# Smaller first pieces of x and of the first weights at the beginning of a two-block transformer kernel

## The chip, the core and the metric

The kernel runs on one core of a Trainium2 chip. The metric is the time of one execution in device microseconds; a profile of one execution shows what each engine did in it. TensorE multiplies, VectorE, ScalarE and GpSimd do the rest, and SyncE here only issues DMAs, as ScalarE and GpSimd can too. A matmul stands in the profile as a weight load (PEld) and a multiplication (PE).

## What is computed

The program is two transformer blocks over 256 rows of 1024 columns. The change touches only the very first product, the input projection of the mLSTM mixer: x (256 x 1024) times the weights `w_in` (1024 x 3080), of which the beginning takes columns 0 to 255 and the eight gate columns.

```python
def mlstm_mixer(x, w_in, gate_b, conv_w, norm_g, w_out):
    proj = x @ w_in
    qk = jax.nn.silu(causal_dwconv(proj[..., :nqk], conv_w))
    v = proj[..., nqk:nqk + nv]
    o = proj[..., nqk + nv:nqk + nv + D_MODEL]
    gates = proj[..., nqk + nv + D_MODEL:].astype(jnp.float32) + gate_b.astype(jnp.float32)
    ...
def first_block(x, mem, mlstm_w_in, ...):
    kv = (mem @ mem_w_kv).astype(jnp.float32)
    ...
            y = mlstm_mixer(x, mlstm_w_in[j], mlstm_gate_b[j], mlstm_conv_w[j],
                            mlstm_norm_g[j], mlstm_w_out[j])
    ...
```

## The kernel before

Every product is split for precision: a factor is rounded to a high part (`WH`, `XH`), and the rest is kept as a low part (`WL`, `XL`); the product is WH·XH + WL·XH + WH·XL, three matmuls for each pair of blocks. The 1024 rows of the contraction are eight blocks of 128. Rounding the high part is a cast, the low part is a subtraction.

All weights come as a list of chunks of 1 MB, each through one of four buffers `RAW`. SyncE issues the chunks in the order of the list; a chunk from number 4 on waits until VectorE has made the low part of the chunk four places ahead. ScalarE casts each chunk (`hi_to`, line 1254), VectorE makes its low part (`lo_to`, line 1948), TensorE multiplies. Each engine's program is written out by hand as a Python function (`tensor`, `scalar`, `vector`, `gpsimd`, `sync`); the engines run their own instructions in order and are tied by counted semaphores.

The beginning is treated apart. x, turned so that its columns lie on partitions (`in_x_t`, into `S`, eight blocks of 256 columns), and chunk 0 of the weights (`in_w_in_first`, into `RAW[0]`, eight blocks of 256) come in four quarters of two blocks, 256 KB each:

- ScalarE issues the first two quarters of the weights (line 1275), SyncE all four of x (line 3073), the gate columns (3075), the last two quarters of the weights (3077), and then chunk 1 (3068).
- ScalarE casts each quarter of x to `XH` (1279), the gate columns to `GH` (1283, 1284), and the last quarter of the weights (1287).
- VectorE casts the first three quarters of the weights (1974), and for each quarter makes the rest of the weights (1978) and the rest of x (1989); once the rest of the gate columns (1984).
- TensorE first runs 15 matmuls on a block of zeros (587), whose product is not used. In `first()` it then takes for each quarter WH·XH, WL·XH, and WH·XL of the quarter before it (`blocks`, line 540, four matmuls each), with the same for the gate columns (`gate`, line 546, two for a quarter; in quarter 1 four, for quarters 0 and 1). That makes 72 matmuls of 256 columns. `second()` follows with chunk 1, in matmuls of 512 columns.

GpSimd loads a mask once the last quarter's rest of x is made (line 2926).

## Time and profile before

| | us |
|---|---|
| median of 3 runs | 938.74 |
| lowest and highest | 938.50, 938.77 |
| the profiled execution | 938.65 |
| its span, first to last instruction | 937.0 |
| TensorE busy | 929.6 |
| VectorE busy | 713.8 |
| ScalarE busy | 528.1 |

The profiled execution lasts 1.65 us longer than its span, since the span leaves out what lies around the instructions. Busy times are sums over the whole span, which has stages of different kinds; which engine sets the end in a stage is read from the waits in it. Times in the views are counted from the span's start. The ends of matmuls are modelled and overlap, so TensorE's pace is read from starts.

### The profile page before, as it was taken

To read this page: it belongs to the slowest core of one execution; us is meant where nothing else is said; L and a number is where in the kernel's file an instruction comes from. 1 tells how busy PE (TensorE), PEld (TensorE's weight loads), DVE (VectorE), ACT (ScalarE), POOL (GpSimd) and SP (SyncE) were. 2 spreads that over 40 slices of the span, in tenths; PEclk is the share of its full clock that TensorE was granted. 3 is DMA by queue.
4 is the path that set the end of the run, shared out by engine and by line. 5 is a ranking of instruction groups with operands and counts; after the bars stand their busy time and mean duration, and the time that the engine had idled before them with its cause. 6 is when DMAs were issued, how large, how long until landed. Compare 5 with 4: busy or idle time off the path is not lost.

```text
span 937.0 us, 12963 instructions
## 1 busy us (share of the span) xinstructions
PE 929.6 (99%) x4989; PEld 801.4 (86%) x4989; DVE 713.8 (76%) x1002; ACT 528.1 (56%) x757; POOL 60.6 (6%) x98
## 2 busy tenths in 40 slices
PE   9999999999999999999999999999999999999997
PEld 8889888988888888889888888888888888888886
DVE  6987778788888776787788877678779886555575
ACT  5867563636655555455275555556576665454543
POOL 0000211001000002100100000002100000000020
PEclk9999999999999999999999999999999999999999
DMA  9795475457988885374399888773733475656521
GB/s 328 235 369 181 135 241 180 164 180 246 321 289 290 287 296 190 105 274 136 130 321 333 288 295 285 252 261 118 247 119 107 136 246 185 221 180 199 173 78 45
DMA packets 109659, 202.98 MB, mean 217 GB/s; under 512 B 4332, under 2 KB 75264, under 8 KB 106272
## 3 DMA queue, kind: packets, MB, share of 16 engines
q1 hardware_dynamic: 106000, 189.15, 59.5%
q0 software_dynamic: 3168, 12.24, 3.8%
q8 instruction: 40, 0.66, 0.3%
q10 hardware_dynamic: 432, 0.79, 0.2%
q14 instruction: 19, 0.16, 0.1%
HBM read 201.09 MB, written 1.06 MB: 216 GB/s over the span
## 4 chain that ended last, share of the span: by engine, by line
PE 98%; DVE 0%; DMA 0%; ACT 0%; issue 0%; POOLq 0%; POOL 0%; ACTq 0%
PE WB L387 23%; PE WB L393 12%; PE YB L414 12%; PE YB L421 12%; PE YB L429 12%; PE YB L490 6%; PE WB L414 3%; PE WB L421 3%; PE WB L429 3%; PE YB L931 1%; PE WB L531 1%; PE WB L789 1%; PE WB L367 1%; PE WB L374 1%; PE WB L370 1%; PE YB L904 1%
## 5 line engine op out<-in xcount | busy, mean ns | idle before, releaser
L1948 DVE TENSOR_TENSOR wl<-raw,wh 128x2048 fp32r<-128x2048 f32 (+1 forms) x143 | 329.0, 2307 | 99.5 <-ACT wh L1254 95.0
L1254 ACT CAST wh<-raw 128x2048 fp32r<-128x2048 f32 (+1 forms) x147 | 280.0, 1907 | 37.1 <-PE YB L429 14.8
L387 PE MATMUL WB<-XS,wh 128*128 128x512 f32 x960 | 230.9, 390 | 0.0
L387 PEld LDWEIGHTS WB<-XS,wh 128*128 128x128 f32 x960 | 178.1, 188 | 36.1 <-DVE U L2619 0.4
L393 PEld LDWEIGHTS WB<-XS,wl 128*128 128x128 f32 x960 | 124.8, 191 | 5.7
L393 PE MATMUL WB<-XS,wl 128*128 128x256 f32 x960 | 126.5, 283 | 0.0
L414 PE MATMUL YB<-wh,FHT 128*128 128x512 f32 x344 | 106.6, 391 | 0.0
L421 PE MATMUL YB<-wl,FHT 128*128 128x512 f32 x344 | 106.2, 390 | 0.0
L429 PE MATMUL YB<-wh,FLT 128*128 128x512 f32 x344 | 106.1, 389 | 0.0
L1479 ACT COPY U<-WB 128x256 f32<-128x256 f32 x102 | 33.1, 376 | 125.8 <-PE WB L393 125.8
L421 PEld LDWEIGHTS YB<-wl,FHT 128*128 128x128 f32 x344 | 64.6, 188 | 13.8
L429 PEld LDWEIGHTS YB<-wh,FLT 128*128 128x128 f32 x344 | 64.6, 188 | 13.7
L414 PEld LDWEIGHTS YB<-wh,FHT 128*128 128x128 f32 x344 | 62.1, 189 | 10.5
L1935 DVE SCALAR_TENSOR_TENSOR raw<-raw,AR 128x1024 f32<-128x1024 f32 x48 | 56.7, 1219 | 0.0
L490 PE MATMUL YB<-wh,XS 128*128 128x512 f32 x160 | 44.2, 402 | 0.0
L414 PE MATMUL YB<-wh,XS 128*128 128x512 f32 x136 | 42.8, 401 | 0.0
L421 PE MATMUL YB<-wl,XS 128*128 128x512 f32 x136 | 41.5, 391 | 0.0
L429 PE MATMUL YB<-wh,XS 128*128 128x512 f32 x136 | 41.4, 390 | 0.0
L1470 ACT CAST XS<-WB 128x512 fp32r<-128x512 f32 x16 | 9.4, 587 | 46.6 <-PE WB L531 46.6
L490 PEld LDWEIGHTS YB<-wh,XS 128*128 128x128 f32 x160 | 28.7, 188 | 6.1 <-DVE XS L2242 0.6
L429 PEld LDWEIGHTS YB<-wh,XS 128*128 128x128 f32 x136 | 25.5, 188 | 5.5
L421 PEld LDWEIGHTS YB<-wl,XS 128*128 128x128 f32 x136 | 25.5, 188 | 5.4
(399 smaller groups left out, 1205.3 us busy)
## 6 DMA issues: line engine op xcount, KB each, us to landing
raw<-in_mlp_w SPq DMA_DIRECT2D x64, 1024.0 KB, 5.4
raw<-in_w_ada_t SPq DMA_DIRECT2D x24, 1024.0 KB, 5.0
raw<-in_mlstm_w_in SPq DMA_DIRECT2D x11, 1024.0 KB, 8.2
raw<-in_w_ffn_down SPq DMA_DIRECT2D x11, 1024.0 KB, 5.1
raw<-in_w_ffn_gate SPq DMA_DIRECT2D x10, 1024.0 KB, 5.4
raw<-in_w_ffn_up SPq DMA_DIRECT2D x10, 1024.0 KB, 5.7
raw<-in_mem_w_kv SPq DMA_DIRECT2D x8, 1024.0 KB, 8.1
raw<-in_xattn_wq SPq DMA_DIRECT2D x8, 1024.0 KB, 7.0
```

The lines of the kernel that those rows point to most:

```text
L367: e.matmul(o, H[:, at(k)], xh[:, k, :], start=k == 0, stop=False)
L387: e.matmul(W[:, :], H[:, at(k, f)], XS[:, k, :], start=k == 0, stop=False)
L393: p = e.matmul(W[:, 0:256], L[:, at(k, f)], XH[:, k, :], start=False, stop=k == 7)
L414: e.matmul(o, xh[:, k0 + k, tk], pick(H, k), start=start and k == 0, stop=False)
L421: f = e.matmul(o, xh[:, k0 + k, tk], pick(L, k), start=False, stop=stop and low_last and k == a - 1)
L429: f = e.matmul(o, xl[:, k0 + k, tk], pick(H, k), start=False, stop=stop and not low_last and k == a - 1)
L490: f = e.matmul(YB[t][:, :], x[:, k, 128 * t:128 * t + 128], w[ms[n] % NS][:, 512 * (k % 4):512 * (k % 4) + 512], start=start and k == 0, s ...
L1254: f = e.copy(w[:, 0:a * b], raw[:, 0:a * b])
L1470: e.copy(XH[:, 4 * h:4 * h + 4, 128 * t:128 * t + 128], W[:, :].rearrange("p (k c) -> p k c", k=4)).then_inc(act_ln.add(("hi", s, t, h)))
L1479: p = e.copy(o[:, 256 * f:256 * f + 256], bank_of.get(key + (f,), WB[0])[:, 256:512])
L1935: f = e.scalar_tensor_tensor(w, w, 1.0, CROW, ALU.mult, ALU.mult, accum_out=MS[:, c:c + 1])
L1948: f = e.tensor_tensor(L[:, 0:a * b], raw[:, 0:a * b], H[:, 0:a * b].bitcast(F32), ALU.subtract)
```

## The change

x and chunk 0 of the weights now land in four pieces of 1, 1, 2 and 4 blocks (`LANDED`) instead of four of 2, and are rounded and multiplied in five parts of 1, 1, 2, 2 and 2 blocks (`ROUNDED`); the last two parts wait for the same landed piece (`lands`).

- ScalarE issues the first three pieces of the weights (128, 128 and 256 KB), SyncE the four of x (128, 128, 256 and 512 KB), the gate columns behind the third, and the last piece of the weights (512 KB) after all of x.
- ScalarE casts x in five parts, the gate columns behind the third, and the weights' blocks 6 and 7. VectorE casts blocks 0 to 5 of the weights in four parts.
- VectorE's order: high and low of part 0, high and low of part 1, rest of x for blocks 0 and 1 in one operation, high and low of part 2, rest of the gates, rest of x, high and low of part 3, rest of x, low of part 4, rest of x.
- TensorE runs 12 matmuls on zeros instead of 15. In `first()` WH·XL of blocks 0 and 1 follows part 1, and for the gate columns part 2. The 72 matmuls stay.
- GpSimd's load of the mask waits for the fifth part instead of the fourth.

```diff
+        LANDED = (slice(0, 1), slice(1, 2), slice(2, 4), slice(4, 8))
+        ROUNDED = (slice(0, 1), slice(1, 2), slice(2, 4), slice(4, 6), slice(6, 8))
+        lands = (0, 1, 2, 3, 3)
...
-                for q in range(4):
-                    ks = range(2 * q, 2 * q + 2)
+                for q, part in enumerate(ROUNDED):
+                    ks = range(part.start, part.stop)
                     e.wait_ge(*act_front["x", q])
-                    e.wait_ge(*(dve_front["w", q] if q < 3 else w_hi[0]))
+                    e.wait_ge(*(dve_front["w", q] if q < 4 else w_hi[0]))
                     blocks(Ws, 0, WH, XH, ks, start=True)
...
-                    if q > 0:
+                    if q == 1:
+                        e.wait_ge(*dve_front["x", 1])
+                        blocks(Ws, 0, WH, XL, range(0, 2))
+                    if q == 2:
+                        gate(GH, XL, range(0, 2))
+                    if q > 2:
+                        ks = range(ROUNDED[q - 1].start, ROUNDED[q - 1].stop)
                         e.wait_ge(*dve_front["x", q - 1])
-                        blocks(Ws, 0, WH, XL, range(2 * q - 2, 2 * q))
-                        gate(GH, XL, range(2 * q - 2, 2 * q))
...
-            for n in range(15):
+            for n in range(12):
                 p = e.matmul(WB[3][:, 0:256], XL[:, 7, 0:128], XL[:, 7, :], start=True, stop=True)
...
-            for q in range(2):
-                e.dma_start(first_quarter(q), I["w_in_first"][:, 2 * q:2 * q + 2, :]).then_inc(d_first[q], 16)
-            for q in range(4):
-                ks, cs = slice(2 * q, 2 * q + 2), slice(512 * q, 512 * q + 512)
-                e.wait_ge(d_xt[q], 16)
+            for q in range(3):
+                e.dma_start(first_part(LANDED[q]), I["w_in_first"][:, LANDED[q], :]).then_inc(d_first[q], 16)
+            for q, ks in enumerate(ROUNDED):
+                e.wait_ge(d_xt[lands[q]], 16)
                 e.copy(XH[:, ks, :], S[:, ks, :]).then_inc(act_front.add(("x", q)))
...
+            def first_high(q):
+                cs = slice(256 * ROUNDED[q].start, 256 * ROUNDED[q].stop)
+                e.wait_ge(d_first[lands[q]], 16)
+                e.tensor_copy(WH[0][:, cs], RAW[0][:, cs]).then_inc(dve_front.add(("w", q)))
...
-            for q in range(4):
-                ks = slice(2 * q, 2 * q + 2)
+            for q, ks in enumerate(LANDED):
                 e.dma_start(S[:, ks, :], I["x_t"][:, ks, :]).then_inc(d_xt[q], 16)
-                if q == 1:
+                if q == 2:
                     e.dma_start(PC[:, C_WG:C_WG + 64], I["gates"]).then_inc(d_gcols, 16)
-                if q > 1:
-                    e.dma_start(first_quarter(q), I["w_in_first"][:, ks, :]).then_inc(d_first[q], 16)
+            e.dma_start(first_part(LANDED[3]), I["w_in_first"][:, LANDED[3], :]).then_inc(d_first[3], 16)
```

SyncE's DMAs from the start up to chunk 1 (`in_mlstm_w_in`), before:

```order
L3073 DMA S<-in_x_t 128x512 x2
L3075 DMA PC<-in_gates 128x64
L3073 DMA S<-in_x_t 128x512
L3077 DMA raw<-in_w_in_first 128x512
L3073 DMA S<-in_x_t 128x512
L3077 DMA raw<-in_w_in_first 128x512
L3068 DMA raw<-in_mlstm_w_in 128x8x256
```

and now:

```order
L3094 DMA S<-in_x_t 128x256 x2
L3094 DMA S<-in_x_t 128x512
L3096 DMA PC<-in_gates 128x64
L3094 DMA S<-in_x_t 128x1024
L3097 DMA raw<-in_w_in_first 128x1024
L3090 DMA raw<-in_mlstm_w_in 128x8x256
```

The weights of blocks 4 and 5 stood ahead of the last quarter of x; now they are in one DMA with blocks 6 and 7, behind all of x.

VectorE from its first cast of the weights (wh) to the cast of blocks 4 and 5, with what each waits for (`in_first` and `raw_in0` are landings of the weights), before:

```order
L1974 CAST wh<-raw 128x512 [waits in_first0]
L1978 TENSOR_TENSOR wl<-raw,wh 128x512 [waits dve_front]
L1989 TENSOR_TENSOR XS<-S,XS 128x2x256 [waits act_front]
L1974 CAST wh<-raw 128x512 [waits in_first1]
L1978 TENSOR_TENSOR wl<-raw,wh 128x512 [waits dve_front]
L1984 TENSOR_TENSOR FLT<-PC,FHT 128x8x4 [waits act_front]
L1984 TENSOR_TENSOR FLT<-PC,FHT 128x8x4
L1989 TENSOR_TENSOR XS<-S,XS 128x2x256
L1974 CAST wh<-raw 128x512 [waits in_first2]
```

and now:

```order
L1981 CAST wh<-raw 128x256 [waits in_first0]
L1986 TENSOR_TENSOR wl<-raw,wh 128x256 [waits dve_front]
L1981 CAST wh<-raw 128x256 [waits in_first1]
L1986 TENSOR_TENSOR wl<-raw,wh 128x256 [waits dve_front]
L1991 TENSOR_TENSOR XS<-S,XS 128x2x256 [waits act_front]
L1981 CAST wh<-raw 128x512 [waits in_first2]
L1986 TENSOR_TENSOR wl<-raw,wh 128x512 [waits dve_front]
L2003 TENSOR_TENSOR FLT<-PC,FHT 128x8x4 [waits act_front]
L2003 TENSOR_TENSOR FLT<-PC,FHT 128x8x4
L1991 TENSOR_TENSOR XS<-S,XS 128x2x256 [waits act_front]
L1981 CAST wh<-raw 128x512 [waits raw_in0]
```

The first cast of the weights is half as wide, the rest of x comes behind two parts of the weights, and the cast of blocks 4 and 5 now waits for the last landing of chunk 0 (`raw_in0`).

TensorE from the matmuls on zeros up to block 4 (wh and wl are the weights' parts, FHT and FLT those of the gate columns), before:

```order
L587 MATMUL WB<-XS 128x256 x15
L540 MATMUL YB<-XS,wh 128x256 x4
L540 MATMUL YB<-XS,wl 128x256 x4
L540 MATMUL YB<-XS,wh 128x256 x4
L546 MATMUL YB<-XS,FHT 64x256 x4
L540 MATMUL YB<-XS,wl 128x256 x4
L546 MATMUL YB<-XS,FLT 64x256 x4
L540 MATMUL YB<-XS,wh 128x256 x4
L546 MATMUL YB<-XS,FHT 64x256 x2
L540 MATMUL YB<-XS,wh 128x256 x4
```

and now:

```order
L596 MATMUL WB<-XS 128x256 x12
L543 MATMUL YB<-XS,wh 128x256 x2
L543 MATMUL YB<-XS,wl 128x256 x2
L543 MATMUL YB<-XS,wh 128x256 x2
L543 MATMUL YB<-XS,wl 128x256 x2
L543 MATMUL YB<-XS,wh 128x256 x8
L549 MATMUL YB<-XS,FHT 64x256 x4
L543 MATMUL YB<-XS,wl 128x256 x4
L549 MATMUL YB<-XS,FLT 64x256 x4
L549 MATMUL YB<-XS,FHT 64x256 x2
L543 MATMUL YB<-XS,wh 128x256 x4
```

Blocks 0 and 1 are now taken one by one, and the low part of x for them (the first four of the row of eight) comes ahead of blocks 2 and 3. In both, the last row is WH·XH of blocks 4 and 5, with 30 matmuls between the zeros and it.

## Rows read from the trace of the kernel before

**Rows 1.** The page, part 1: busy time of each engine, share, instructions.

```profile
PE 929.6 (99%) x4989; PEld 801.4 (86%) x4989; DVE 713.8 (76%) x1002; ACT 528.1 (56%) x757; POOL 60.6 (6%) x98
```

**Rows 2.** The waits of TensorE, whole span: us in total, times, longest.

```profile
PE WB L587 <- DVE XS L1964: 1.2, 1, 1.2
PE YB L540 <- DVE wh L1974: 0.2, 1, 0.2
```

**Rows 3.** The chain that ended last, 0 to 15 us: start, us, what.

```profile
0.73 3.58 DMA raw<-in_w_in_first
4.34 0.44 DVE wh L1974
4.91 2.61 PE YB L540 x12
...
14.11 0.48 PE YB L540 x4
```

**Rows 4.** Stretches, TensorE: us, busy (instructions), granted clock, DMA share, GB/s.

```profile
5.00:7.00 2.00, 2.00 (x10) 1.00 0.97 298
7.00:9.48 2.48, 2.48 (x22) 1.00 1.01 355
```

**Rows 5.** Weight loads by line, 1:4.6 and 7.8:14 us: xcount, busy, mean ns.

```profile
L587 PEld LDWEIGHTS WB<-XS 128*128 128x128 f32 x15 | 3.3, 327 | 1.2 <-DVE XS L1964 1.2
...
L540 PEld LDWEIGHTS YB<-XS,wh 128*128 128x128 f32 x22 | 3.0, 189 | 0.0
```

**Rows 6.** The timeline of weight loads: start, us, instruction, count.

```profile
5.69 0.97 PEld L540 LDWEIGHTS YB<-XS,wl 128*128 128x128 f32 x4
6.55 0.76 PEld L540 LDWEIGHTS YB<-XS,wh 128*128 128x128 f32 x4
```

**Rows 7.** The timeline of TensorE, two pieces of it.

```profile
9.48 0.63 PE L540 MATMUL YB<-XS,wh 128*128 128x256 f32 x4
...
14.43 3.82 PE L540 MATMUL WB<-XS,wh 128*128 128x512 f32 x16
```

**Rows 8.** The timeline of SyncE: when each DMA is issued.

```profile
2.57 0.43 SPq L3077 DMA_DIRECT2D raw<-in_w_in_first  x1
...
3.51 0.43 SPq L3077 DMA_DIRECT2D raw<-in_w_in_first  x1
```

**Rows 9.** DMAs in flight from 0.9, 1.3, 2.8, 3.7 us: KB, us to landing.

```profile
raw<-in_w_in_first ACTq DMA_DIRECT2D x1, 256.0 KB, 3.6
...
raw<-in_w_in_first ACTq DMA_DIRECT2D x1, 256.0 KB, 4.4
...
raw<-in_w_in_first SPq DMA_DIRECT2D x1, 256.0 KB, 5.5
...
raw<-in_w_in_first SPq DMA_DIRECT2D x1, 256.0 KB, 5.9
```

**Rows 10.** The timeline of VectorE, the casts and rests of the first blocks.

```profile
4.34 0.43 DVE L1974 CAST wh<-raw 128x512 fp32r<-128x512 f32 x1 [1.81 <-DMA raw<-in_w_in_first]
4.80 0.69 DVE L1978 TENSOR_TENSOR wl<-raw,wh 128x512 fp32r<-128x512 f32 x1
...
8.09 0.43 DVE L1974 CAST wh<-raw 128x512 fp32r<-128x512 f32 x1
```

**Rows 11.** Packets of all queues in 2.1:5.6, 5:5.6, 5.8:9.5, 9.5:12.4 us.

```profile
DMA packets 747, 1.14 MB, mean 325 GB/s; under 512 B 208, under 2 KB 208, under 8 KB 747
...
DMA packets 137, 0.13 MB, mean 225 GB/s; under 512 B 79, under 2 KB 79, under 8 KB 137
...
DMA packets 889, 1.29 MB, mean 348 GB/s; under 512 B 62, under 2 KB 459, under 8 KB 889
...
DMA packets 1102, 1.06 MB, mean 365 GB/s; under 512 B 32, under 2 KB 1102, under 8 KB 1102
```

**Rows 12.** The timeline of ScalarE, the last cast of chunk 0 and chunk 1.

```profile
9.48 0.62 ACT L1287 CAST wh<-raw 128x512 fp32r<-128x512 f32 x1
...
13.39 1.04 ACT L1292 CAST wh<-raw 128x1024 fp32r<-128x1024 f32 x1
```

More of the change, by code:

```diff
@@ L551, in first @@
                 Ws = [YB[f][:, 0:256] for f in range(2)]
-                for q in range(4):
-                    ks = range(2 * q, 2 * q + 2)
+                for q, part in enumerate(ROUNDED):
+                    ks = range(part.start, part.stop)
                     e.wait_ge(*act_front["x", q])
-                    e.wait_ge(*(dve_front["w", q] if q < 3 else w_hi[0]))
+                    e.wait_ge(*(dve_front["w", q] if q < 4 else w_hi[0]))
                     blocks(Ws, 0, WH, XH, ks, start=True)
-                    gs = range(0 if q == 1 else 2 * q, 2 * q + 2)
-                    if q > 0:
+                    gs = range(0 if q == 2 else part.start, part.stop)
+                    if q > 1:
                         e.wait_ge(*act_front["gates"])
                         gate(GH, XH, gs, start=True)
-                    e.wait_ge(*(w_lo0[q] if q < 3 else w_lo[0]))
+                    e.wait_ge(*(w_lo0[q] if q < 4 else w_lo[0]))
                     blocks(Ws, 0, WL, XH, ks)
-                    if q > 0:
+                    if q > 1:
                         e.wait_ge(*dve_front["gates"])
                         gate(GL, XH, gs)
-                    if q > 0:
+                    if q == 1:
[5 more added lines that the diff above has]
+                        ks = range(ROUNDED[q - 1].start, ROUNDED[q - 1].stop)
                         e.wait_ge(*dve_front["x", q - 1])
-                        blocks(Ws, 0, WH, XL, range(2 * q - 2, 2 * q))
-                        gate(GH, XL, range(2 * q - 2, 2 * q))
-                e.wait_ge(*dve_front["x", 3])
+                        blocks(Ws, 0, WH, XL, ks)
+                        gate(GH, XL, ks)
+                e.wait_ge(*dve_front["x", 4])
                 gate(GH, XL, range(6, 8), stop=True).then_inc(pe_front.add("gates"))
@@ L1978, in vector, with first_low, x_low @@
+            def first_low(q):
+                cs = slice(256 * ROUNDED[q].start, 256 * ROUNDED[q].stop)
+                e.wait_ge(*(dve_front["w", q] if q < 4 else w_hi[0]))
                 e.tensor_tensor(WL[0][:, cs], RAW[0][:, cs], WH[0][:, cs].bitcast(F32), ALU.subtract
-                                ).then_inc(w_lo0.add(q) if q < 3 else w_lo.add(0))
+                                ).then_inc(w_lo0.add(q) if q < 4 else w_lo.add(0))
+            def x_low(q, ks):
                 e.wait_ge(*act_front["x", q])
-                if q == 1:
-                    e.wait_ge(*act_front["gates"])
-                    for o, c in ((0, 0), (32, 4)):
-                        p = e.tensor_tensor(GL[:, :, o:o + 4], GRAW[:, :, c:c + 4], GH[:, :, o:o + 4].bitcast(F32),
-                                            ALU.subtract)
-                    p.then_inc(dve_front.add("gates"))
@@ L1987, in vector @@
-                if q == 3:
-                    e.wait_ge(*pe_front["zeros"])
                 e.tensor_tensor(XL[:, ks, :], S[:, ks, :], XH[:, ks, :].bitcast(F32), ALU.subtract
                                 ).then_inc(dve_front.add(("x", q)))
+            first_high(0)
+            first_low(0)
+            first_high(1)
+            first_low(1)
+            x_low(1, slice(0, 2))
+            first_high(2)
+            first_low(2)
+            e.wait_ge(*act_front["gates"])
+            for o, c in ((0, 0), (32, 4)):
+                p = e.tensor_tensor(GL[:, :, o:o + 4], GRAW[:, :, c:c + 4], GH[:, :, o:o + 4].bitcast(F32),
+                                    ALU.subtract)
@@ L1991, in vector @@
+            p.then_inc(dve_front.add("gates"))
+            x_low(2, slice(2, 4))
+            first_high(3)
+            first_low(3)
+            x_low(3, slice(4, 6))
+            first_low(4)
+            e.wait_ge(*pe_front["zeros"])
+            x_low(4, slice(6, 8))
             at[:] = [1, 1]
```

22 lines of the change are left out of this document (7 added, 15 removed).

## The prediction

> **What bounds the kernel now.** I read the page first, then who waited for whom, then the first 20 us piece by piece. The page says that TensorE is busy 99% of the span [rows 1]. That is an average, so I asked what TensorE ever waits for in the 937.0 us: two waits, 1.2 us for the first memset and 0.2 us for the first cast weights [rows 2]. After the first true matmul at 4.91 us it never waits again. So from there the end moves by exactly as much as TensorE's stream is shifted, and nothing later takes a shift back. The question is only where the stream stands when the work of `first()` is over.
>
> The chain at the start [rows 3]: the first quarter of the weights is issued at 0.73 and lands about 3.6 us later, VectorE casts it from 4.34 to 4.78, and the first true matmul starts at 4.91. Then matmuls run back to back into the second chunk, whose first one starts at 14.43 [rows 7]. Their pace has two levels. The granted-clock column prints 1.00 in all these stretches, though 10 matmuls stand in the two microseconds up to 7.0 and 22 in the next 2.5 [rows 4], but the weight loads took 327 ns on average while the 15 dummy matmuls ran and 189 ns after 7.8 us [rows 5], and four load-and-multiply pairs took 0.86 us (the loads that start at 5.69 and at 6.55, [rows 6]) and later 0.47 us [rows 3]: 0.215 against 0.1175 us each. That is 1.2 GHz up to about 7.0 us and 2.4 GHz from there.
>
> So TensorE's order matters in a second way: up to 9.48 it does 30 matmuls (8 of quarter 0, 22 of quarter 1 with the gate columns), and 42 after that (from 9.48 to 14.43, 4.95 us, [rows 7]). At 9.48 it turns to blocks 4 and 5. In the kernel before these had landed with margin: their weights are issued at 2.57 [rows 8] and land 5.5 us later [rows 9], at 8.07; VectorE's cast starts at 8.09 [rows 10]; TensorE wants it at 9.48.
>
> **The change, part by part.**
>
> *Small first pieces.* x and the first weights of block 0 are 128 KB each instead of 256 KB. Before, the first 256 KB of the weights landed 3.6 us after the issue [rows 9], those of x a little earlier. Between 2.1 and 5.6 us all queues together moved 325 GB/s [rows 11], so 256 KB less ahead of the first wait is 0.8 us at most; if the landing is latency and not bytes, it is nothing. I take 0.7. VectorE's cast of 256 columns instead of 512 saves about half of 0.43 us [rows 10], say 0.15. The first true matmul then starts at 4.91 - 0.85 = 4.05, between 3.9 and 4.91. The lower end is set by the dummies: 12 instead of 15 takes 3 x 0.215 = 0.65 us off their end, from about 4.55 to 3.9.
>
> *The order on TensorE.* Blocks 0 and 1 now come singly; the same 30 matmuls stand ahead of blocks 4 and 5 as before (4 + 8 + 18), and 42 stand behind. From 4.05 at the slow step up to 7.0 that is 13 or 14 matmuls, and 16 at 0.1175 follow: TensorE is through with them at 8.9 to 9.0. With a start at 4.91 it would be 9.48 again.
>
> *The order on VectorE.* The second part of x's remainder is now one operation over blocks 0 and 1 after both weight parts. From 3.6 on its row is cast 0 (0.25), rest 0 (0.35), then cast 1 from its landing near 4.35, rest 1 and x rest (0.69 as any of these rests, [rows 10]), which ends near 5.7; TensorE asks for it after 8 matmuls, 4.05 + 8 x 0.215 = 5.77. The cast of blocks 2 and 3 then runs to 6.2 and TensorE wants it at 6.6, since w(2:4) lands as w(1) did before, near 5.6 (issued at 1.2, 4.4 us to landing, [rows 9]). These are all covered, the first by under 0.1 us; that cover gone, it costs the same few tenths, but only ahead of the wait that follows, and so nothing.
>
> *The large last pieces.* Here the change adds a wait. The weights of blocks 4 to 7 are one 512 KB piece, and it stands last of the six DMAs of the beginning on SyncE's queue. Before, blocks 4 and 5 of the weights came ahead of x's last quarter. Now VectorE's cast of them, which TensorE needs at 8.9, waits until blocks 6 and 7 have come as well. The same bytes lie ahead of that last byte as before (1 MB of x, 1 MB of weights, the gates; 512 KB of them on ScalarE's queue in both), and before it landed 5.9 us after its issue at 3.51, at 9.4 [rows 8, 9]. ScalarE's cast of it started at 9.48 [rows 12].
>
> How early can it land now? One bound is the old one, 9.4, or 0.1 to 0.2 later. For the other: in 5.0 to 5.6 the queues moved only 225 GB/s, in 5.8 to 9.5 348, and once one chunk streamed undisturbed, 365 [rows 11]. If the dip and the piece boundaries vanish, 0.6 x 225 + 3.6 x 348 = 1390 KB at 365 GB/s are 3.8 us, so 5.0 + 3.8 = 8.8. There are fewer and longer pieces behind 5.6 us (two of 512 KB where there were four of 256 KB), but the gates' small packets are still there. I take the middle, 9.1.
>
> From landing to matmul the row of the first quarter gives the price: landed 4.33, cast from 4.34, matmul at 4.91 [rows 3, 10], 0.58 us. So blocks 4 and 5 begin at 9.1 + 0.58 = 9.7 instead of 9.48. TensorE stands idle from 8.9 to 9.7. The 0.5 us that the early start brings are given back in that wait, and 0.2 us more.
>
> *Behind the wait.* Queued behind VectorE's waiting cast are its rests of w(4:6), x(4:6), w(6:8) and x(6:8), 0.69 us each [rows 10]: they end at 9.1 + 0.45 + 4 x 0.7 = 12.4. TensorE asks for the first at 9.7 + 6 x 0.1175 = 10.4 (it is there at 10.25), for w(6:8) at 12.5 (there at 11.7) and for the last x at 13.9. All hold. ScalarE casts w(6:8) from 9.2 to 9.8; needed at 11.8. The second chunk's cast, whose second half runs from 13.39 to 14.43 [rows 12], is not later, since its bytes are not; TensorE comes to the first half near 14.6 and to the second 1.8 later.
>
> *What else is moved.* SyncE issues six DMAs ahead of the second chunk instead of seven, so that one is issued some 0.5 us earlier; it queues behind the same bytes, so I count nothing. GpSimd's mask load waits for the last x rest, now some 1 us later; its reader comes tens of us later.
>
> **The sum.** The profiled execution took 938.65 us with a span of 937.0; the median of the runs is 938.74. Shift of TensorE's stream at blocks 4 and 5: 9.7 - 9.48 = +0.2 us; everything behind it moves along: 938.65 + 0.2 = 938.85, or 938.94 from the median. I say 938.9. The bounds of the landing, 8.8 and 9.6, make -0.1 and +0.7; the lower one stops at TensorE's own readiness (8.9 to 9.48); neither leaves 938.5 to 939.4.
>
> **Rivals.**
>
> *The large piece lands early.* If it lands by 8.4, TensorE at 8.95 finds its weights and the whole early start is kept: 9.48 - 8.95 = 0.53 us, 938.1. For it speaks the dip to 225 GB/s, which is lost time between small pieces; against it that even at 365 GB/s throughout I come only to 8.8, which keeps nothing or 0.1. The Trainium skill, "DMA: Bandwidth & Descriptors", Rules for kernel authors, asks for DMAs of 1 MiB or more for the greatest bandwidth; by that rule the long pieces would land early and the short ones late. The rows only show that the rate was higher later, not that the size did it. Chance 0.2 for some gain between 0.1 and 0.5.
>
> *Slower: TensorE's clock falls in the new wait.* The place is the 0.8 us of idleness at 8.9, the first after the rise. If the chip takes it for idleness, the matmuls behind it run at 0.215 again. At the start the low level lasted from 1.2 to 7.0, 5.8 us [rows 2, 4]: in such a stretch 27 matmuls run that would take 3.2 us, so +2.6 and 941.5, slower by 0.3%. It decides from a wait long enough to count, of which no row of before tells, as TensorE never waits there once it is at 2.4 GHz. The Trainium skill, "TensorE: Matmul & The Clock Gate", What's actually happening, says that "the default state is throttled, and activity releases the throttle"; no run here shows a fall in mid-kernel. The wait is short beside the 5.8 us of the rise: chance 0.04. A rise that only comes later than 7.0 costs less, as the wait at 8.9 hides most of it.
>
> *The first pieces land no earlier.* Then the first matmul stays at 4.91, the dummies end 0.65 us earlier into an idle engine, and the 30 matmuls end at 9.48: TensorE still waits until 9.7, and the time is the same 938.9. Chance 0.1; it cannot be told from the forecast by the time, only by the trace.
>
> **How the numbers follow.** Forecast 0.66 at 938.9 (own range 938.5 to 939.4), no earlier landing 0.1 at the same time, gain 0.2 down to 938.1, clock 0.04 at 941.5. The range of 938.1 to 939.5 leaves out the clock case and the tails. A measurement of this kernel can tell about 0.2%, 1.9 us, from no change; every case but the clock's is inside, so: same 0.95, slower 0.04, faster 0.01.
>
> **What would show it.** In the profile after: the first true matmul near 4.05 with a cast of 256 columns ahead of it; a wait of TensorE for the cast of blocks 4 and 5, 0.5 to 1 us long, ending near 9.7, released by VectorE, whose cast in turn waits for the DMA of the first weights; no other wait of TensorE; matmuls at 0.1175 us behind it; the second chunk's first matmul near 14.65 instead of 14.43. I am wrong if the last weight piece lands well before 9.0, if TensorE waits for x's or the weights' rests, or if the loads behind the wait take 327 ns again.

## The result, and the profile after

| | before | after |
|---|---|---|
| median of 9 runs each, us | 938.50 | 942.20 |
| lowest and highest | 938.38, 938.77 | 940.03, 943.71 |
| ratio, 95% interval | | 1.0033 (1.0025 to 1.0042) |
| the profiled execution | 938.65 | 943.71 |

The change makes the kernel slower by 3.7 us in the median. The ratio is estimated from all the runs; the two medians alone would give 1.0039. The forecast was 938.9, with 938.1 to 939.5 as its range; none of the nine runs lies in it. The nine runs after fall into two groups: four at 940.03 to 940.42 with a mean granted clock of 0.998 or more, and five at 942.20 to 943.71 with 0.996 or 0.997. One profile was taken in each group; the second belongs to another execution of the same kernel, told below as e13. One of the ten runs of e15 below took 1323.94 us at a mean granted clock of 0.655, and is in neither its median nor its ratio.

The page of the slower execution, busy time of each engine, which answers to [rows 1]:

```profile
PE 931.6 (99%) x4986; PEld 803.5 (85%) x4986; DVE 714.1 (76%) x1004; ACT 528.4 (56%) x758; POOL 61.0 (6%) x98
```

Its waits of TensorE over the whole span (us in total, times, longest), which answer to [rows 2]:

```profile
PE YB L543 <- ACT FHT L1292: 3.2, 1, 3.2
PE WB L596 <- DVE XS L1972: 1.2, 1, 1.2
```

The shares are within a point of those before. What is new is one line, 3.2 us of waiting in line 543, for ScalarE's cast of the gate columns. The timeline of TensorE (start, us, instruction, count) says where, and answers to [rows 7]:

```profile
3.91 0.77 PE L543 MATMUL YB<-XS,wh 128*128 128x256 f32 x2
...
5.66 0.67 PE L543 MATMUL YB<-XS,wh 128*128 128x256 f32 x4
9.56 1.19 PE L543 MATMUL YB<-XS,wh 128*128 128x256 f32 x4 [3.23 <-ACT FHT L1292]
...
13.53 1.05 PE L543 MATMUL YB<-XS,wh 128*128 128x256 f32 x4
...
19.48 1.78 PE L543 MATMUL WB<-XS,wh 128*128 128x512 f32 x7
```

The first true matmul is at 3.91. After twelve matmuls, all that blocks 0 and 1 give, TensorE has nothing, from 6.3 to 9.56: it waits ahead of blocks 2 and 3, not ahead of blocks 4 and 5, which begin at 13.53. `second()` starts at 19.48 instead of 14.43, 5.05 us late, and the execution ends 943.71 - 938.65 = 5.06 us late.

Who is late there is told first by the chain that ended last (start, us, what), which answers to [rows 3]:

```profile
2.09 7.04 DMA PC<-in_gates
9.14 0.02 issue
9.16 0.22 ACT FHT L1291
```

Then by the timeline of VectorE, its casts of the first weights, of blocks 2 and 3, and of blocks 4 and 5 [rows 10]:

```profile
3.47 0.29 DVE L1981 CAST wh<-raw 128x256 fp32r<-128x256 f32 x1 [0.94 <-DMA raw<-in_w_in_first]
...
8.98 0.43 DVE L1981 CAST wh<-raw 128x512 fp32r<-128x512 f32 x1 [3.44 <-DMA raw<-in_w_in_first]
...
11.74 0.43 DVE L1981 CAST wh<-raw 128x512 fp32r<-128x512 f32 x1 [0.80 <-DMA raw<-in_w_in_first]
```

And by the DMAs of x(2:4), w(2:4), the gate columns and w(4:8), with their KB and us from issue to landing [rows 9]:

```profile
S<-in_x_t SPq DMA_DIRECT2D x1, 256.0 KB, 5.5
raw<-in_w_in_first ACTq DMA_DIRECT2D x1, 256.0 KB, 7.3
PC<-in_gates SPq DMA_DIRECT2D x1, 32.0 KB, 7.0
...
raw<-in_w_in_first SPq DMA_DIRECT2D x1, 512.0 KB, 8.7
```

The weights of blocks 2 and 3 take 7.3 us to land, the gate columns 7.0. The second quarter of the weights, which held the same blocks, took 4.4 [rows 9]. The last piece of the weights takes 8.7 us and lands at 11.71, where the last quarter took 5.9 and landed at 9.46. A landing is sixteen arrivals, each of which counts the DMA's semaphore up by one, and an engine that waits for the count of 16 needs the last. Of the weights of blocks 2 and 3, ten arrivals are in by 5.44, and the other six come at 6.13, 6.36, 6.76, 7.29, 8.38 and 8.96. Before, all sixteen came between 4.97 and 5.58.

Behind the wait the matmuls are slow. Two stretches (us, then busy and count of PE, PEld, DVE, ACT and POOL, then granted clock, DMA share, GB/s), which answer to [rows 4]:

```profile
9.56:15.67 6.11, 6.11 (x29) 6.11 (x30) 4.31 (x9) 2.71 (x5) 0.33 (x1) 0.50 1.09 361
15.95:19.48 3.53, 3.53 (x33) 3.53 (x32) 2.29 (x1) 0.76 (x1) 0.17 (x1) 1.00 1.10 362
```

A group of weight loads in the first of them (count, busy, mean ns), which answers to [rows 5]:

```profile
L543 PEld LDWEIGHTS YB<-XS,wl 128*128 128x128 f32 x8 | 1.9, 330 | 0.0
```

The granted clock is 0.50 in the first stretch, that is 1.2 GHz, and a load takes 330 ns, as the dummy matmuls' loads did before. In the record the clock falls at 8.93, while TensorE still waits, and is back at 15.76. So two things add up. Had the clock stayed, the 18 matmuls of blocks 2 and 3 and the gates would have ended at 9.56 + 18 x 0.1175 = 11.7. Blocks 4 and 5 would have had to wait for their landing, 11.71 + 0.58 = 12.3, and with 42 matmuls in 5.0 us `second()` would have started at 17.3. Of the 5.05 us, then, 2.9 belong to the landings and 2.2 to the clock. This division is worked out, not measured; e11 and e13 show a fall and a late landing each by itself.

### The profile page after: what moved, and what is told of

Read it like the earlier page. It is cut to its first block, busy times and chain, and to the rows that moved or that the text cites. A ratio compares the mean times of both kernels' runs of the same rounds, so it can differ in the third digit from the quotient of the medians.

```text
span 941.9 us, 12960 instructions
## 1 busy us (share of the span) xinstructions
PE 931.6 (99%) x4986; PEld 803.5 (85%) x4986; DVE 714.1 (76%) x1004; ACT 528.4 (56%) x758; POOL 61.0 (6%) x98
## 4 chain that ended last, share of the span: by engine, by line
PE 98%; DMA 1%; DVE 0%; ACT 0%; issue 0%; SPq 0%; POOLq 0%; POOL 0%; ACTq 0%
PE WB L390 23%; PE WB L396 12%; PE YB L417 12%; PE YB L424 12%; PE YB L432 12%; PE YB L493 6%; PE WB L417 3%; PE WB L424 3%; PE WB L432 3%; PE YB L940 1%; PE WB L534 1%; PE WB L798 1%; PE WB L370 1%; PE WB L377 1%; PE WB L373 1%; DMA PC<-in_gates 1%
```

## The experiments

All are compared with the kernel before on the same chips (938.3 to 938.6 in the median). "After" is the changed kernel. The table gives for each profiled execution when the latest of x(2:4), w(2:4) and the gate columns landed (what `first()` needs for its third part), when the last piece of the weights landed, how much all queues moved from 5.0 to 7.5 us, and when `second()` began; then the median of the runs and the ratio with its interval. One profile is one execution, and landings scatter; the medians carry the verdicts.

| kernel | blocks 2, 3 and gates | last weights | GB/s | `second()` | median | ratio |
|---|---|---|---|---|---|---|
| before | 5.84 | 9.46 | 295 | 14.43 | 938.50 | |
| after | 9.14 | 11.71 | 200 | 19.48 | 942.20 | 1.0033 (1.0025, 1.0042) |
| e13 after, again | 6.64 | 10.31 | 227 | 15.93 | 940.15 (one run) | |
| e1 last pieces split | 7.60 | 10.01 | 270 | 16.66 | 939.93 | 1.0016 (1.0006, 1.0025) |
| e2 before, last joined | 7.48 | 10.27 | 210 | 15.88 | 940.15 | 1.0018 (1.0009, 1.0028) |
| e3 matmuls in the wait | 9.48 | 12.12 | 236 | 17.72 | 941.56 | 1.0032 (1.0020, 1.0044) |
| e4 chunk 1 later | 8.03 | 10.62 | 291 | 16.23 | 941.32 | 1.0028 (1.0017, 1.0039) |
| e5 gates by GpSimd | 9.55 | 11.78 | 202 | 19.53 | 944.00 | 1.0059 (1.0044, 1.0074) |
| e6 w(4:8) ahead of x(4:8) | 6.85 | 8.88 | 227 | 15.88 | 940.80 | 1.0027 (1.0018, 1.0037) |
| e7 e1 and e5 together | 7.30 | 9.82 | 307 | 15.02 | 941.84 | 1.0038 (1.0024, 1.0052) |
| e8 x contiguous | 6.50 | 9.81 | 336 | 15.43 | 939.78 | 1.0015 (1.0005, 1.0024) |
| e12 weights contiguous | 7.66 | 10.12 | 293 | 15.74 | 940.03 | 1.0017 (1.0007, 1.0026) |
| e14 both contiguous | 7.20 | 9.93 | 360 | 15.54 | 939.69 | 1.0013 (1.0003, 1.0023) |
| e9 both contiguous, split | 6.85 | 9.42 | 346 | 14.39 | 939.50 | 1.0011 (1.0001, 1.0020) |
| e15 w(2:4) by SyncE | 7.39 | 10.40 | 221 | 16.02 | 940.36 | 1.0024 (1.0014, 1.0033) |
| e10 before, contiguous | 6.95 | 9.41 | 312 | 14.98 | 938.56 | 1.0001 (0.9991, 1.0010) |

In all of these profiles but e1's (0.4) and e9's (0.9), the delay of `second()` against 14.43 agrees within 0.2 us with the delay of the whole execution against 938.65.

### Each half of the change alone: e1 and e2

e1 is after with the last piece cut in two again, so that the small first pieces stand alone.

```diff
-        LANDED = (slice(0, 1), slice(1, 2), slice(2, 4), slice(4, 8))
+        LANDED = (slice(0, 1), slice(1, 2), slice(2, 4), slice(4, 6), slice(6, 8))
...
-        lands = (0, 1, 2, 3, 3)
+        lands = (0, 1, 2, 3, 4)
...
+                if q > 2:
+                    e.dma_start(first_part(ks), I["w_in_first"][:, ks, :]).then_inc(d_first[q], 16)
-            e.dma_start(first_part(LANDED[3]), I["w_in_first"][:, LANDED[3], :]).then_inc(d_first[3], 16)
```

> The changed kernel with its last pieces of four blocks cut into two of two blocks, each with a wait of its own, in the order x(4:6), w(4:6), x(6:8), w(6:8); all else stays. In the profile of the changed kernel the bytes moved fell to 85 to 250 GB/s from 5.0 to 7.5 us, just when x's 512 KB piece began, and blocks 2 and 3 and the gate columns landed at 7.1 to 9.1 us. Theory A (the 512 KB piece of x with its rows of 4 KB fills the rings and slows them): blocks 2 and 3 land near 5.6 again, TensorE waits nowhere after 3.9, the clock does not fall, 938.0 us (0.5 below before). Theory B (chunk 1's DMA, issued 0.5 us earlier, disturbs): here it is issued as late as before, so also near 938. Theory C (the small first pieces, or the third piece of the weights on ScalarE's queue, upset the rings): blocks 2 and 3 land as late as now, 940 to 943 us.

e2 is the kernel before with only its last two quarters joined, of x and of the weights.

```diff
-            for q in range(4):
-                ks = slice(2 * q, 2 * q + 2)
+            for q in range(3):
+                ks = slice(2 * q, 2 * q + 2) if q < 2 else slice(4, 8)
                 e.dma_start(S[:, ks, :], I["x_t"][:, ks, :]).then_inc(d_xt[q], 16)
...
```

> The kernel before with only its last two quarters of x and of the weights joined into pieces of four blocks (512 KB); the first two quarters, the 15 matmuls on zeros and all orders stay. Theory A: the slow stretch comes at 5 to 7.5 us here too; but only what lies behind the first two quarters is late: the weights of blocks 4 to 7 land near 11, TensorE waits about 1 to 2 us at 9.5 us, 940 to 942 us. Theory C: the slow stretch stays away, the last weights land near 9.4, 939.0 to 939.3 us (the wait that the prediction worked out).

Each half costs by itself: 939.93 and 940.15. For e1 theories A and B gave 938.0; it did not come, though there is no large piece in e1 and chunk 1 is issued at 4.48 us, later than before. Seven of its ten runs are at 939.30 to 940.23, the other three at 941.08 to 941.45 with a mean clock of 0.996 or 0.997. e2 came out at the lower end of theory A's 940 to 942, with the joined weights earlier than its 11 us. In e1 TensorE's wait stands at blocks 2 and 3; in e2 it stands once at the gate columns and once at blocks 4 and 5. The waits of TensorE in e1, but for the first memset's:

```profile
PE YB L543 <- DVE wh L1981: 1.3, 1, 1.3
```

And those in e2:

```profile
PE YB L540 <- DVE wh L1974: 0.8, 2, 0.7
PE YB L546 <- ACT FHT L1284: 0.6, 1, 0.6
```

In e2 nothing ahead of the joined pieces was touched, and yet two of the sixteen arrivals of the gate columns came at 7.20 and 7.48, where fourteen had come by 5.83; and the joined weights landed at 10.27, 0.8 later than the last quarter did. So the joining, as e2 does it, neither brings the last piece sooner nor leaves the pieces ahead of it alone. But chunk 1 has two DMAs fewer ahead of it in e2 and is issued at 3.05 instead of 3.99; what the joining does without that is not shown by e2. e4 below holds chunk 1 back in the changed kernel.

### The clock: e3 and e11

e3 fills the wait of after with 24 matmuls on zeros between parts 1 and 2, whose product is not used.

```diff
+                    if q == 2:
+                        for n in range(24):
+                            p = e.matmul(WB[3][:, 0:256], XL[:, 7, 0:128], XL[:, 7, :], start=True, stop=True)
+                        p.then_inc(pe_front.add("zeros"))
                     e.wait_ge(*act_front["x", q])
...
-            p.then_inc(pe_front.add("zeros"))
```

> The changed kernel with 24 more matmuls on zeros between part 1 and part 2, where TensorE stood idle for 3.2 us in its profile. They change no landing. If half of the loss is the clock that falls in the idle stretch (matmuls of 0.2135 us from 8.9 to 15.8 us in the profile, 34 of them instead of 0.1175: some 2.2 to 3 us), the slowest runs of 942 to 944 us go and all lie near 940 to 941. If the clock is no part of it, the spread of 940 to 944 us stays.

The gate columns landed as late as in after's first profile (9.48), but the clock record stays at 1.00 from its rise to the last microseconds, and no run is above 942.03. The last weights landed at 12.12, and `second()` began at 17.72, which is 12.12 + 0.58 + 5.0: the landings' share as worked out above, without the clock's. The zeros themselves cost 24 x 0.1175 = 2.8 us in runs that would not have waited so long, so the lowest run rises from 940.03 to 940.92, and nothing is won on the whole: the ratio is 1.0032 against 1.0033.

e11 is the kernel before with one wait put in: TensorE waits for the landing of chunk 1 ahead of blocks 4 and 5. No DMA is changed.

```diff
                 for q in range(4):
                     ks = range(2 * q, 2 * q + 2)
+                    if q == 2:
+                        e.wait_ge(s_raw[1], 16)
```

> The kernel before with one more wait on TensorE: ahead of blocks 4 and 5 it waits for the landing of chunk 1, at 12.4 us in the profile of before, so it stands idle from 9.5 to about 12.5 while every landing stays as it is. It prices idleness by itself. If the clock stays at 2.4 GHz: 3.1 us, 941.5. If the clock falls in it, matmuls of 0.2135 us follow for some microseconds and the weight loads there take 327 ns: 943 to 945 us, with a spread between runs of 2 us or more.

Its wait of TensorE for chunk 1:

```profile
PE YB L540 <- DMA raw<-in_mlstm_w_in: 3.5, 1, 3.5
```

The stretch behind it, with the granted clock third from the end:

```profile
12.63:18.50 5.87, 5.87 (x27) 5.87 (x28) 2.29 (x1) 1.97 (x2) 0.35 (x1) 0.50 1.10 356
```

And the first matmuls of `second()` in the timeline of TensorE:

```profile
20.37 0.86 PE L540 MATMUL WB<-XS,wh 128*128 128x512 f32 x3
```

Blocks 4 and 5 begin at 12.63 instead of 9.48, so idleness alone is 3.15 us, and 938.5 + 3.15 = 941.65. One of the four runs is there (941.50, clock 0.998). Two are at 943.37 and 944.64 with 0.996 and 0.995; the fourth is at 943.21 with 0.998, and has no profile that would tell why. In the profiled one `second()` is 20.37 - 14.43 = 5.94 us late, 2.8 more than the wait explains. That is the price of the fall by itself, in a kernel whose DMAs are those of before.

### The changed kernel again: e13

> The changed kernel itself, a second look. If late landing of blocks 2 and 3 is its habit, the profile shows TensorE waiting there again, 1 to 3.5 us, with w(2:4) or the gate columns landing at 7.4 or later, and the time is 940 to 940.5 without a fall of the clock and 942 to 944 with one. If the first profile was an odd execution, the wait at blocks 2 and 3 is under 0.5 us and the main wait stands at blocks 4 and 5, 1 to 1.5 us.

Its wait of TensorE, beside that for the memset:

```profile
PE YB L543 <- DVE wh L1981: 1.5, 1, 1.5
```

Its timeline of TensorE, from the first true matmul to `second()`:

```profile
4.01 0.77 PE L543 MATMUL YB<-XS,wh 128*128 128x256 f32 x2
...
8.98 0.39 PE L549 MATMUL YB<-XS,FHT 128*64 128x256 f32 x2
10.91 0.71 PE L543 MATMUL YB<-XS,wh 128*128 128x256 f32 x4 [1.53 <-DVE wh L1981]
...
15.93 3.82 PE L543 MATMUL WB<-XS,wh 128*128 128x512 f32 x16
```

And the stretch from blocks 4 and 5 to `second()`, at a granted clock of 1.00:

```profile
10.91:15.93 5.02, 5.02 (x43) 5.02 (x43) 2.93 (x5) 2.04 (x3) 0.78 (x1) 1.00 1.10 352
```

This is the forecast's own course with one number changed. The matmuls run through blocks 2 and 3 with a pause of 0.13 us by the profile (0.33 by the starts). TensorE is through with the thirty at 9.2, and waits for blocks 4 and 5 alone. Their weights land at 10.31 instead of 9.1, the matmul follows 0.60 later, the clock stays, and the execution is 940.15, 1.5 us slower than before's. Of my two branches the second held: the main wait stands at blocks 4 and 5, with 1.53 us where 1 to 1.5 were expected. The time alone would have fitted the first as well. So the 1.6 us of the four runs without a fall can come from either place.

### What makes the landings late: e4, e5, e6, e7 and e15

Five changes in what stands beside the late pieces. e4 holds back chunk 1, e5 takes the gate columns' short rows off SyncE's queue, e6 sends the weights ahead of x, e7 is e5 with the pieces of e1 and has no further edit, e15 moves w(2:4) from ScalarE's queue to SyncE's.

```diff
+            e.wait_ge(d_xt[3], 16)
             for n in range(1, len(chunks)):
```

> The changed kernel with one more wait on SyncE: chunk 1 and all behind it are issued only when x's last piece has landed. Theory A and C: the slow stretch from 5 to 7.5 us stays, blocks 2 and 3 land late as now, 940 to 943 us, or worse by what chunk 1 is late. Theory B (chunk 1's 1024 short rows per partition group, made ready from 4 us on, slow the rings): the stretch goes, blocks 2 and 3 land near 5.6, the last weights near 9.2, about 939 us.

```diff
-                if q == 2:
-                    e.dma_start(PC[:, C_WG:C_WG + 64], I["gates"]).then_inc(d_gcols, 16)
...
+            e.dma_start(PC[:, C_WG:C_WG + 64], I["gates"]).then_inc(d_gcols, 16)
             e.memset(MH, -0.5).then_inc(po_front.add("mh"))
```

> The changed kernel with the gate columns' DMA (128 rows of 256 bytes) taken out of SyncE's queue: GpSimd issues it at the very start. In every trace so far the packets turn slow at 5.0 us, just when this DMA has run. Theory G (the short rows disturb the rings): the slow stretch at 5 to 7.5 us goes or moves to 3 us, blocks 2 and 3 land by 5.6, and the time falls to 938 to 939 us. Theory X (x's last blocks are read slowly whatever stands ahead): slow packets stay from 5 to 7.5 us, but the gates land early; TensorE still waits for blocks 2 and 3 or for 4 and 5, 939.5 to 942 us. Theory T (something else runs at that time): as X.

```diff
             for q, ks in enumerate(LANDED):
+                if q == 3:
+                    e.dma_start(first_part(ks), I["w_in_first"][:, ks, :]).then_inc(d_first[q], 16)
                 e.dma_start(S[:, ks, :], I["x_t"][:, ks, :]).then_inc(d_xt[q], 16)
...
-            e.dma_start(first_part(LANDED[3]), I["w_in_first"][:, LANDED[3], :]).then_inc(d_first[3], 16)
```

> The changed kernel with the two 512 KB pieces in the other order, weights of blocks 4 to 7 first, then x's. Theory X (reading x is what is slow): the stretch from 5 us runs near 380 GB/s now, and the slow stretch comes behind it, at about 6.3 to 8; blocks 2 and 3 land near 5.6, TensorE then waits for x's blocks 4 and 5 at about 9.5 to 10.5. Theory G and T: the weights' packets are slow from 5 to 7.5 us as x's were, blocks 2 and 3 land at 7 to 9 us, 940 to 943 us.

> Both at once: the last pieces in two of two blocks each, and the gate columns issued by GpSimd. If each of the two (long pieces, short rows) delays the landings by itself, this is the one of the four that beats the kernel before: no wait of TensorE behind 3.9 us, 938.0 us. If the slow stretch has another cause, it waits for blocks 2 and 3 as in the run with the split pieces alone, 939 to 941.5 us.

```diff
-            for q in range(3):
+            for q in range(2):
                 e.dma_start(first_part(LANDED[q]), I["w_in_first"][:, LANDED[q], :]).then_inc(d_first[q], 16)
...
                 if q == 2:
+                    e.dma_start(first_part(ks), I["w_in_first"][:, ks, :]).then_inc(d_first[q], 16)
                     e.dma_start(PC[:, C_WG:C_WG + 64], I["gates"]).then_inc(d_gcols, 16)
```

> The changed kernel with the weights of blocks 2 and 3 issued by SyncE behind x(2:4) instead of by ScalarE. If its place in the row of transfers made it late (ScalarE issues it before x(2:4), and its packets then share the engines with x(2:4) and x(4:8)), it lands within 0.3 us of x(2:4), near 7.1, and the wait shrinks to about 1.3 us: 939.8 to 940.3 and no fall. If the slow stretch of the engines takes whatever is in flight between 5 and 7.5 us, w(2:4) lands at 7.4 to 9 as before and the time stays 940 to 943.

None of the five brings the landings back, so none of these neighbours is the cause by itself. In e4 the queues moved more in the slow stretch, but one of the sixteen arrivals came at 7.31, 8.03 and 10.62 for w(2:4), the gates and w(4:8), 1.1 to 1.7 us behind the fifteenth each time: a better mean rate, the same wait. In e5 the gate columns were in earlier (7.30), and four of the sixteen arrivals of x(2:4) came at 8.42 to 9.07; TensorE waited 3.8 us, the clock fell at 8.30, and all four runs are above 943.7. In e6 the weights landed at 8.88, and then x(4:8) was the late one, at 10.14. e7 shows both pictures in its runs: 939.29 in the profiled one, and 941.50 to 942.70 with a clock of 0.996 or 0.997 in the four others. In e15 x(2:4) was in at 5.54 and w(2:4), right behind it, at 7.20, since one arrival came a full microsecond after the others (6.22). Seven of e15's runs are at 940.03 to 940.68, two at 942.26 and 942.74.

### How the pieces lie in HBM: e8, e12, e14, e9 and e10

In HBM a partition of x and of the first weights is a row of eight blocks, 8 KB, of which a DMA of four blocks reads 4 KB. In these kernels each piece is an array of its own, so that a DMA reads one closed stretch. e8 does it for x, e12 for the first weights, e14 for both, e9 for both with the five pieces of e1, e10 for both in the kernel before. The edit of e8, the others being like it:

```diff
-                e.dma_start(S[:, ks, :], I["x_t"][:, ks, :]).then_inc(d_xt[q], 16)
+                e.dma_start(S[:, ks, :], I[f"x_t{q}"]).then_inc(d_xt[q], 16)
...
+    for q, (a, b) in enumerate(((0, 1), (1, 2), (2, 4), (4, 8))):
+        out[f"x_t{q}"] = out["x_t"][:, a:b]
+    del out["x_t"]
```

> The changed kernel with x laid out in four arrays, one for each landed piece, so that a piece is read as one contiguous stretch instead of 128 rows 8 KB apart; nothing else changes. Theory X with the rows' distance as its cause: x's pieces run at the full rate, blocks 2 and 3 land near 5.6, 938 to 939 us. If the distance has no part in it: 940 to 943 us as the changed kernel.

> The changed kernel with the first weights (and not x) laid out piece by piece. If it is the reads of x alone that turn slow in the changed kernel, this changes nothing: 940 to 943.5 us, blocks 2 and 3 at 7 to 9 us. If any of the two read contiguously spares the other (they share the DMA engines), it comes down as with x alone, to about 939.8 us with one wait for the 512 KB piece.

> The changed kernel with x and the first weights stored as four contiguous arrays each. If the strided rows make the lag of the landings, both waits shrink: no wait at blocks 2 and 3, and at blocks 4 and 5 the forecast's 0.8 us with w(4:8) landing near 9.1; time 938.7 to 939.2. If it is the number and size of pieces whatever their layout, w(4:8) lands at 9.8 or later as with x alone in pieces, and the time is 939.6 to 940.

> The changed kernel with five landed pieces (1, 1, 2, 2, 2 blocks) and both x and the first weights laid out piece by piece, each piece one contiguous stretch to read. With x alone laid out so, blocks 2 and 3 landed at 6.05 us instead of 7.1 to 9.1 and TensorE waited only for the 512 KB piece of the weights. Theory L (the change loses only by late landings, of blocks 2 and 3 through slow reads and of 4 and 5 through the large piece): no wait of TensorE behind 3.9 us, or one under 0.3; 937.8 to 938.2 us, below before. If slow reads come back with the split pieces: 939 to 941 us.

> The kernel before with x and the first weights laid out quarter by quarter, contiguous; nothing else. It tells what the layout is worth by itself. TensorE waits nowhere behind 4.9 us in the kernel before, so earlier landings of later quarters change nothing: 938.2 to 938.7 us, as before. If the first quarter lands earlier too, up to 0.3 us less.

The packets of all queues from 5.0 to 7.5 us in before (count, MB, rate, and how many are small):

```profile
DMA packets 467, 0.74 MB, mean 295 GB/s; under 512 B 115, under 2 KB 115, under 8 KB 467
```

In after:

```profile
DMA packets 258, 0.50 MB, mean 200 GB/s; under 512 B 113, under 2 KB 113, under 8 KB 258
```

In e2:

```profile
DMA packets 258, 0.53 MB, mean 210 GB/s; under 512 B 133, under 2 KB 133, under 8 KB 258
```

In e8:

```profile
DMA packets 381, 0.84 MB, mean 336 GB/s; under 512 B 160, under 2 KB 160, under 8 KB 381
```

In e14:

```profile
DMA packets 434, 0.90 MB, mean 360 GB/s; under 512 B 170, under 2 KB 170, under 8 KB 434
```

Before moves 0.74 MB in this stretch, after 0.50. The seven profiles with a joined last piece out of strided rows and chunk 1 right behind move 200 to 236 GB/s; the changed kernels with x contiguous (e8, e14, e9) move 336 to 360. So the layout counts for the rate, but the rate does not hang on it alone: the strided quarters of before move 295 (266 in e11, which has the same DMAs), e4 with chunk 1 held back 291, e12 with only the weights contiguous 293, and e10 with all contiguous 312. The Trainium skill, "DMA: Bandwidth & Descriptors", Latency and other measured facts, tells of copies whose rows lie a large power of two apart in HBM, with 207 GB/s at a pitch of 512 KiB and 103 at 4 MiB, and names contiguous tiles as one remedy. The pitch here is 8 KB, and no run here shows whether that is the same effect.

But the time comes back only in part. In e8 TensorE waits no longer than 0.2 us at a time up to blocks 2 and 3, and one long wait is left, 1.4 us, since the weights of blocks 4 to 7 land at 9.81. The timeline of TensorE in e8:

```profile
10.41 0.71 PE L543 MATMUL YB<-XS,wh 128*128 128x256 f32 x4 [1.41 <-DVE wh L1981]
```

In e14 the rate is the best of all, and TensorE still waits 1.1 us at blocks 2 and 3 and 0.6 us at blocks 4 and 5, as the last arrivals of w(2:4) and w(4:8) come at 7.03 and 9.93, where the first come at 5.46 and 8.30. My expectation for strided rows as the whole cause falls with it. e12, with only the weights contiguous, keeps both waits, 1.2 us at blocks 2 and 3 and 0.3 us at blocks 4 and 5, with a median of 940.03; but it too moves more than after (293), so the rows of x are not the only ones that count. What the layout changes most is how often the clock falls: of the thirty runs of e8, e12 and e9 none has a mean clock under 0.998, of e14's ten two have 0.997. Against after's four runs without a fall (940.03 to 940.42) the medians of e8, e12 and e14 win 0.5 us at the most; the larger part of the distance to after's 942.20 is falls that do not come.

e9, with the smaller pieces, is the best of the changed kernels and still 1.05 us above before in the median. Its waits of TensorE, but for the first memset's:

```profile
PE YB L543 <- ACT XS L1287: 0.8, 1, 0.8
PE WB L534 <- DVE X L2332: 0.3, 1, 0.3
```

Theory L fails with the first of them, which stands at blocks 2 and 3. Yet `second()` begins at 14.39, as early as in before: the clock had risen at 5.34 here and at 7.01 there. The 0.9 us that this execution is longer lie behind the beginning, 0.4 of them at the second wait, at 399.42 us, which no other profile has. No run shows whether the change has a part in that, so what makes up e9's 1.05 us is open.

e10 shows the margin of the old order: there too one arrival straggles (blocks 2, 3 and gates at 6.95, 0.7 us of waiting, 939.38 in that execution), and the median is the same as before's. No kernel of the fifteen is faster than before.

Three pieces stay open. What makes single arrivals straggle, most of all between 5 and 9.5 us, isn't settled: chunk 1, the gate columns, the order of x and weights and the queue are not it alone, and the layout is only a part. What e1's small first pieces do wrong is not taken apart: no run has only the smaller DMAs, or only the shorter row of zeros. And why the last joined piece lands later than the last quarter in every kernel that has it at the end of the queue (9.81 to 12.12 against 9.46) is told by no run: the first of its sixteen arrivals is hardly later (8.23 to 8.87 against 8.32).

## Why the prediction was wrong

*What bounds the kernel* held. The stream of TensorE is shifted as a whole: in after's first profile each later matmul of TensorE starts 5.03 to 5.09 us behind its place in before, from 26 us to the end, and in e13 1.44 to 1.54. Nothing takes a shift back.

*Small first pieces* held. The first true matmul is at 3.91 and, in e13, at 4.01; 4.05 was forecast, from a cast of 0.29 us where 0.28 was worked out.

*The order on VectorE* failed at "w(2:4) lands as w(1) did before, near 5.6 ... These are all covered". It landed at 8.96 and in e13 at 6.44, the gate columns at 9.14 and 6.64. The slip is in the transfer of a landing from one program to another: I took 4.4 us from a row of before and gave it to a DMA which is issued later and has other company. w(1) was the second DMA on ScalarE's queue, w(2:4) is the third, as the issues on that queue show, in before and then in after:

```profile
0.73 0.89 ACTq L1275 DMA_DIRECT2D raw<-in_w_in_first  x2
0.73 1.37 ACTq L1284 DMA_DIRECT2D raw<-in_w_in_first  x3
```

The third is issued at 1.65, not at 1.2. With the same 4.4 us it lands at 6.05, as it does in e8, and no profile with these pieces has it earlier. And the cover was thin: 0.4 us between the 6.2 and the 6.6 that I worked out. In e13 TensorE was ready for blocks 2 and 3 at 6.7, near the forecast's 6.6; in after's first profile, where the clock rose at 5.52 instead of near 7.0, it was through with blocks 0 and 1 before 6.3, and the cover had gone too. What a landing then lags is waited for in full.

*The large last pieces* held as a mechanism and failed as a size. "I take the middle, 9.1" measured 10.31 in e13 and 9.81 in e8, both above my upper bound of 9.6. My lower bound was added up wrongly besides: 0.6 + 3.6 us from 5.0 end at 9.2 and not at the 9.4 of the old landing; with 3.8 us it would have been 9.0 instead of 8.8. The step from landing to matmul, 0.58, measured 0.60 in each. The bounds came from mean rates, how long all the bytes take together. The wait ends with the last arrival: in e13 the sixteen arrivals reach from 8.28 to 10.31, in before's last quarter from 8.32 to 9.46. A sum by the mean rate can't see that. The joining was also meant to leave the rate alone or to raise it; with it the rate was 200 or 227 GB/s in the stretch in question, and 295 before. Chunk 1, issued 0.5 us earlier, was counted for nothing; in e4, which holds it back, the rate is 291, but the waits stay. With the 10.31 in its place the forecast's sum gives 10.31 + 0.58 - 9.48 = +1.4, and e13 has +1.5.

*The rival of the clock* was the right mechanism with too small a chance. I gave it 0.04 at 941.5, from a wait of 0.8 us. It came in five of nine runs, as their mean clocks tell. The argument for the small chance, that the wait is short beside the 5.8 us of the rise, failed: the wait was 3.2 us in after, and in e1 a fall followed one of 1.3. Its price was put at 2.6 us; it is 2.2 in after's profile by the working above, less than the 29 slow matmuls would cost (29 x 0.0975 = 2.8), as 0.6 us of it lie in a wait for blocks 4 and 5 that is there anyway; in e11 it is 2.8. The Trainium skill, "TensorE: Matmul & The Clock Gate", What's actually happening, was quoted for the throttled state as the default; a fall in mid-kernel, which no row of before could show, is now shown at 8.93 in after and at 11.80 in e11.

*The rival of the early large piece*, with a chance of 0.2, has no run on its side. The Trainium skill's rule that I named with it ("DMA: Bandwidth & Descriptors", Rules for kernel authors) speaks of DMAs of 1 MiB and more, and no piece of x or of the first weights is that large, so it isn't put to the test. What the runs show is that all queues together moved less with the pieces doubled to 512 KB (e2 beside before, 210 and 295 GB/s), and that the last weights came later.

So the course of events was foreseen for the first 5 us, the sum was wrong by its landings, and the waits that these made were followed by the fall of the clock in five of the nine runs. Of the signs that the prediction named for being wrong, the slow loads came in after's first profile. In e13 none came, and the time was still outside the range: a landing behind 9.6 was not among them.

## What to carry to other kernels

Before transfers are cut, joined or used earlier, ask of each piece how long before its use the last of its sixteen arrivals came, because an earlier start and a joined piece both eat that margin. A landing time belongs to its neighbours in the queues; for a moved or resized DMA take its bounds from the last arrival, not from the mean rate, and its issue from the new queue, and let the range reach over a straggler of one to three microseconds. Where a new wait of TensorE may grow past a microsecond, price the slow clock behind it into the range.

## What the runs showed that I had not expected

- The wait's length alone doesn't tell whether the clock falls. In e1 a wait of 1.27 us, which ended at 7.99, was followed by a fall at 8.18; in e13 a wait of 1.53 us was not. In e1 the clock had risen at 4.76, in e13 at 6.95. The stretch of e1 behind its wait:

```profile
7.99:11.30 3.31, 3.31 (x16) 3.31 (x17) 3.28 (x8) 1.84 (x4) 0.00 (x0) 0.53 1.07 374
```

- The same kernel lands the same DMA at 8.96 and at 6.44 in two executions, and its runs scatter over 3.7 us where the nine of before scatter over 0.4. Of the 88 runs of before that stand beside the experiments one took 940.41, the others 938.11 to 939.18. A kernel with margin at its landings hides most of that scatter; one without shows it.
- Joining two DMAs of 256 KB into one of 512 KB, for x and for the weights, went with 0.53 MB instead of 0.74 in the 2.5 us concerned (e2), and storing x in closed pieces with 0.84 (e8).
- The clock's rise at the start scatters from 4.58 us (e8) to 7.01 (before) over the seventeen profiles, though TensorE's first matmul starts at 1.17 or 1.18 in each; in e11, whose beginning is that of before, it came at 4.98. The 7.0 from which the prediction worked out when TensorE is ready was one value of that scatter.
